# Router logits from four column groups and heads' squares added by GpSimd in the mix stage of an encoder layer

## The chip, the cores and the metric

One Trainium2 chip, of which the kernel uses one core. The metric is device time in microseconds (us) of one execution. TensorE works through matrix products, VectorE and ScalarE through elementwise work, GpSimd through elementwise work beside them, SyncE issues most transfers. TensorE's clock has two levels, 1.2 and 2.4 GHz; the profile gives the granted clock as a share of the upper one.

## The reference, cut to what matters

One layer of a hybrid encoder: 1024 tokens of 1024 channels, three mixers (Hyena, RG-LRU, 8 heads of attention), whose outputs are normalised, joined and projected; a residual and a layer norm; then 16 experts, each of which picks its best 128 tokens.

```python
y = concatenate([_rms_norm(y_hy, gn[:g0]), _rms_norm(y_lr, gn[g0:g1]), _rms_norm(y_at, gn[g1:])], axis=-1)
x = _layer_norm(alpha * x + y @ w_out[l], ln_mix_g[l], ln_mix_b[l])
...
affinity = softmax(einsum("bsd,de->bse", x, router_w), axis=-1)   # 1024 channels to 16 experts
gate, idx = top_k(swapaxes(affinity, 1, 2), cap)
```

The change touches the second and the fourth of these lines: how the mean square of the heads' output `y_at` is formed, and how the logits `x @ router_w` are.

## The kernel before

The program is one block for each engine, written in order by hand, with semaphores between the engines. No scheduler moves anything. Memory is one arena with places by number.

The **mix stage** goes over the 1024 tokens in 8 tiles of 128 (`for i in range(TT)` in each engine's block). For tile i TensorE does, in this order:

- 24 products of 128x512 for the Hyena and LRU channels into banks 0 and 1 (L1516 to L1518, `mix`). Each fp32 product is made of three products of rounded halves (high x high, high x low, low x high), so 4 slices x 2 halves of the columns x 3.
- the turning of the finished row of tile i-1 (`x1_turn`, L1494, 8 transposes into banks 4 and 5).
- the sum of squares of the heads' output of tile i: four fp32 products of the squares `o_sq` (128 x 128 each) with a column of ones into column i of bank 7 (L1539).
- 24 products for the heads' channels into banks 2 and 3 (`mix` again).
- the router logits of tile i-1 (`logits`, L1507): 8 fp32 products with the turned row `x1T` as weights (128 columns) and 16 moving columns of the router's matrix `rw`.

An fp32 product stands as two records in the trace, a rounded one as one.

ScalarE makes the rounded high part of the heads' output of tile i+2 and its squares (`heads_out`, L949 and L950), the roots, the router's exponential, the copies of turned rows, and starts the accumulator. GpSimd multiplies and shifts the residual row of the tile (`residual`, L619 and L620, after its transfer has landed) and forms the low part of the heads' output (`heads_out_low`, L613). VectorE adds the residual to banks 0 and 1 (L2033), adds the heads' banks 2 and 3 scaled (L2046; L2057 in two halves for the last tile), takes the statistics, and applies the norm in two steps with a tensor from memory each (L2052 with the gain, L2053 with the shift). The finished row x1 goes to memory and to `x1_turn`, and only after it does SyncE issue the transfer of the residual row two tiles on (L514). Since the buffers are double, tile i+1's residual follows tile i-1's finished row.

In the last tile the heads' products come in two halves of the columns, and its logits follow the turning of its row. Then VectorE picks the tokens (about 37 us) and the experts begin.

Of the kernel before, what the change touches and what calls it, by code (L numbers as in the profile page):

```python
# [8 lines left out]
ALU = mybir.AluOpType  # L9
ACT = mybir.ActivationFunctionType  # L10
# [71 lines left out]
def encoder(nc, A, out):  # L82

    ctx = ExitStack()
    with ctx:
        def sem(name):
            return ctx.enter_context(nc.semaphore(name))
# [134 lines left out]
        rw = mem(52176, KT, NE)  # L222
# [57 lines left out]
        s_x1st, s_acst, s_acc = [sem(f"x1_stored{i}") for i in range(2)], [sem(f"acc_stored{i}") for i in range(2)], sem("acc_scaled")  # L280
        s_x1p, s_x1ta, s_x1tv, s_lg = sem("x1_turned"), sem("x1T_act"), sem("x1T_dve"), sem("logits")
# [115 lines left out]
        def _(sp):  # L397
# [98 lines left out]
            sp.dma_start(rw, rows(A["router_w"][0])).then_inc(s_rw, 16)  # L496
# [44 lines left out]
        def _(pool):  # L541
# [72 lines left out]

            def residual(i):

                res = xres[:, i % 2, :]
                pool.wait_ge(s_xh[i % 2], 32 + 16 * (i // 2 + 1))
                link(pool.tensor_tensor(res, res, gin, ALU.mult))  # L619
                pool.tensor_tensor(res, res, bin_, ALU.add).then_inc(s_res, 1)  # L620

            pool.wait_ge(s_gb, 32)
            residual(0)
            heads_out_low(0)
            heads_out_low(1)
            residual(1)
            for i in range(2, TT):
                residual(i)
                heads_out_low(i)

# [56 lines left out]
        def _(act):  # L687
# [283 lines left out]

            def mix_root(i):

                act.wait_ge(s_st, TT + i + 1)
                a(sd[:, i % 2:i % 2 + 1], mv[:, i % 2, 1:2], ACT.Sqrt, bias=eps).then_inc(s_sd, 1)
# [10 lines left out]
            for i in range(TT):  # L986
                if i:
                    x1_copy(i - 1)
                heads_root(i)
                if i >= 2:  # L990
                    router_exp(i - 2)
                if i + 2 < TT:
                    heads_out(i + 2)
                mix_root(i)
                if i + 1 < TT:
                    acc_start(i)
# [65 lines left out]
        def _(pe):  # L1062
# [433 lines left out]

            def logits(i):

                if i == 0:
                    pe.wait_ge(s_rw, 48 + 16)  # L1500
                else:
                    pe.wait_ge(s_re, i)
                pe.wait_ge(s_x1ta, i + 1)
                for k in range(KT):
                    if k == KT // 2:
                        pe.wait_ge(s_x1tv, i + 1)
                    ins = mm(bank(6)[:, NE * (i % 2):NE * (i % 2) + NE], x1T[i % 2][:, P * k:P * k + P], rw[:, k, :], start=(k == 0), stop=(k == KT - 1))  # L1507
                ins.then_inc(s_lg, 1)
# [16 lines left out]
            for i in range(TT):  # L1525
# [7 lines left out]
                pe.wait_ge(s_sq, SUMS + i + 1)  # L1533
# [4 lines left out]
                for c in range(4):  # L1538
                    ins = mm(bank(7)[:, i:i + 1], o_sq[:, i % 2, c, :], ones[:, 0:1], start=(c == 0), stop=(c == 3))  # L1539
                ins.then_inc(s_ssq, 1)  # L1540
# [3 lines left out]
                if i + 1 < TT:  # L1544
                    for c in range(4):
                        ins = mix(2, 4 + c, ya_hi[:, i % 2, c, :], ya_lo[:, i % 2, c, :], c == 0, c == 3)
                    ins.then_inc(s_mix, 1)
                else:
                    for j in range(2):
                        for c in range(4):  # L1550
                            ins = mix_half(2, j, 4 + c, ya_hi[:, i % 2, c, :], ya_lo[:, i % 2, c, :], c == 0, c == 3)
                        ins.then_inc(s_mix, 1)
                if i:
                    logits(i - 1)
# [633 lines left out]
```

## Time and profile before

| | us |
|---|---|
| median of 3 runs | 1585.96 |
| lowest and highest | 1584.27, 1586.00 |
| the profiled execution, device time | 1584.54 |
| its span | 1582.7 |
| the mix stage in it | about 819 to 945 |
| the experts' stage in it | about 990 to the end |

Mean granted clock 0.98. TensorE is busy 95% of the span, VectorE 63%, ScalarE 46%, GpSimd 26%. In a timeline a row gives the start, the duration, the engine, the line and the operation; neighbours of one line are drawn together with their count, and the square bracket tells how long the engine was idle before and what ended that. Because records of TensorE overlap, the time of one is read from the distance of the starts. A record of VectorE or GpSimd includes what it waits for once it has begun.

### The profile page before, as it was taken

The page shows a single profiled execution, that of the slowest core. Times are in us where ns is not written, and L with a number is a line of the kernel's source. Part 1 is how long each engine was busy: PE and PEld are TensorE (multiplying, and loading weights), DVE is VectorE, ACT ScalarE, POOL GpSimd, SP SyncE. Part 2 cuts the span into 40 slices and gives each one's busy share as a digit, 9 for nine tenths or more (in the row PEclk, how much of TensorE's full clock was granted, in tenths as well). Part 3 has the DMA queues.
Part 4 walks back from the last instruction along what each step waited for, and adds up shares of the span by engine and source line. Part 5 has one row for each costly group of instructions (what it writes and reads, how often), then busy time and mean ns, then how long its engine had stood idle before and what let it go on. Part 6 is the DMA issues. An engine that isn't in the chain of part 4 may idle for free.

```text
span 1582.7 us, 15796 instructions
## 1 busy us (share of the span) xinstructions
PE 1497.3 (95%) x5862; PEld 996.5 (63%) x5862; DVE 1003.1 (63%) x1014; ACT 720.9 (46%) x696; POOL 406.3 (26%) x209
## 2 busy tenths in 40 slices
PE   6999999999999999999999970999999999999997
PEld 3444487844344444555558860788888888888774
DVE  4533244442842564655635558699989989998886
ACT  3301000025422114355443341677777777777773
POOL 0031000000011003576673414023322223332204
PEclk9999999999999999999999985999999999999999
DMA  9311030115100000000123249699999999999994
GB/s 315 131 54 53 25 135 1 33 31 116 53 0 1 0 0 27 1 27 1 54 82 104 96 156 378 235 368 377 378 371 375 378 378 378 378 379 368 377 381 195
DMA packets 152886, 284.46 MB, mean 180 GB/s; under 512 B 25300, under 2 KB 35874, under 8 KB 152835
## 3 DMA queue, kind: packets, MB, share of 16 engines
q1 hardware_dynamic: 147219, 263.32, 46.8%
q0 software_dynamic: 4464, 16.25, 3.9%
q10 hardware_dynamic: 1152, 4.19, 0.6%
q8 instruction: 34, 0.56, 0.1%
q14 instruction: 17, 0.14, 0.0%
HBM read 259.10 MB, written 24.64 MB: 179 GB/s over the span
## 4 chain that ended last, share of the span: by engine, by line
PE 85%; DVE 6%; DMA 4%; ACT 2%; issue 2%; POOL 1%; SPq 0%; POOLq 0%; DVEq 0%; ACTq 0%
PE psum L1145 14%; PE psum L1605 9%; PE psum L1607 9%; PE psum L1606 9%; PE psum L1376 4%; PE psum L1238 3%; PE psum L1126 3%; DMA arena<-in_exp_w_down 3%; PE psum L1438 3%; PE psum L1346 3%; PE psum L1426 2%; PE psum L1091 2%; PE psum L1449 2%; PE psum L1427 2%; PE psum L1428 2%; PE psum L1254 2%
## 5 line engine op out<-in xcount | busy, mean ns | idle before, releaser
L2109 DVE TENSOR_TENSOR split_at<-arena,split_at 128x2048 fp32r<-128x2048 f32 x188 | 427.9, 2290 | 60.6 <-ACT split_at L1007 59.7
L1007 ACT ACTIVATE split_at<-arena 128x2048 fp32r<-128x2048 f32 x192 | 367.6, 1915 | 68.5 <-PE psum L1607 53.3
L1605 PE MATMUL psum<-split_at,split_at 128*128 128x512 f32 x768 | 305.9, 398 | 1.4 <-DVE split_at L2115 1.4
L1607 PE MATMUL psum<-split_at,split_at 128*128 128x512 f32 x768 | 300.2, 391 | 0.0
L1606 PE MATMUL psum<-split_at,split_at 128*128 128x512 f32 x768 | 299.5, 390 | 0.0
L1145 PE MATMUL psum<-arena 128*128 128x512 f32 x512 | 224.7, 594 | 1.4 <-DVE arena L1862 1.4
L1145 PEld LDWEIGHTS psum<-arena 128*128 128x128 f32 x512 | 96.1, 190 | 124.0 <-issue 123.9
L1607 PEld LDWEIGHTS psum<-split_at,split_at 128*128 128x128 f32 x768 | 144.5, 188 | 31.2
L1605 PEld LDWEIGHTS psum<-split_at,split_at 128*128 128x128 f32 x768 | 144.7, 188 | 29.7 <-DVE split_at L2115 1.8
L1606 PEld LDWEIGHTS psum<-split_at,split_at 128*128 128x128 f32 x768 | 144.9, 189 | 28.3
L1920 DVE TENSOR_REDUCE arena<-psum 128x1 f32<-128x1024 f32 x64 | 78.1, 1224 | 68.9 <-PE psum L1346 68.2
L639 POOL COPY arena<-arena 128x1 uint32 (+1 forms) x14 | 28.3, 2020 | 359.4 <-DVE arena L2143 359.4
L582 POOL TENSOR_TENSOR arena<-arena 128x1024 f32<-128x1024 f32 x32 | 75.6, 2371 | 170.2 <-ACT arena L889 133.2
L889 ACT ACTIVATE arena<-psum 128x1024 f32<-128x1024 f32 x64 | 65.4, 1022 | 71.4 <-PE psum L1428 71.2
L1376 PE MATMUL psum<-arena 128*128 128x512 f32 x176 | 77.0, 592 | 0.0
L1012 ACT ACTIVATE split_at<-psum 128x512 fp32r<-128x512 f32 x64 | 38.2, 597 | 74.8 <-PE psum L1574 61.6
L1438 PE MATMUL psum<-arena 128*64 128x512 f32 x256 | 60.9, 596 | 0.0
L558 POOL TENSOR_TENSOR arena<-arena 128x1024 f32<-128x1024 f32 x7 | 16.8, 2394 | 167.2 <-ACT arena L816 160.7
L1376 PEld LDWEIGHTS psum<-arena 128*128 128x128 f32 x176 | 33.3, 190 | 40.0 <-issue 39.3
L657 POOL DMA_INDIRECT acc_scratch<-arena x15 | 50.9, 3391 | 28.1 <-DVE arena L2143 25.7
L1238 PE MATMUL psum<-arena 128*128 128x256 f32 x256 | 57.5, 379 | 0.0
L761 ACT ACTIVATE arena<-psum 128x256 f32<-128x256 f32 x8 | 3.1, 383 | 117.0 <-PE psum L1254 103.0
(302 smaller groups left out, 2219.3 us busy)
## 6 DMA issues: line engine op xcount, KB each, us to landing
arena<-in_exp_w_gate SPq DMA_DIRECT2D x64, 1024.0 KB, 14.4
arena<-in_exp_w_up SPq DMA_DIRECT2D x64, 1024.0 KB, 14.2
arena<-in_exp_w_down SPq DMA_DIRECT2D x64, 1024.0 KB, 14.4
arena<-in_w_in SPq DMA_DIRECT2D x9, 1024.0 KB, 8.4
arena<-in_x SPq DMA_DIRECT2D x8, 512.0 KB, 6.6
xhat_scratch<-arena SPq DMA_DIRECT2D x8, 512.0 KB, 10.0
arena<-in_w_out SPq DMA_DIRECT2D x8, 512.0 KB, 3.6
arena<-xhat_scratch SPq DMA_DIRECT2D x8, 512.0 KB, 4.8
```

Source lines behind the costliest of these rows:

```text
L582: pool.tensor_tensor(p_pair[q % 2], p_at[:, b, :], p_at[:, b + 1, :], ALU.add).then_inc(s_pa, 1)
L889: a(p_at[:, n % 4, :], bank(2 * (n % 2), 2), ACT.Exp).then_inc(s_exp, 1)
L1007: a(flat(wsplit[c % WS][0]), wraw[:, c], ACT.Copy).then_inc(s_whi, 1)
L1145: ins = mm(bank(proj_bank(i) + j, 1, p0, p0 + w), win_w[c][:, k, at:at + w], xT[:, k, HALF * j:HALF * j + HALF], start=(k == 0), stop=(k = ...
L1238: ins = mm(bank(4 + f % 2)[:, HYW * part:HYW * part + HYW], mat[:, i, P * f:P * f + P], pm[:, part, i, :], start=(i == 0), stop=(i == 3))
L1376: ins = mm(bank(heads_bank(u) + j), w[:, k, P * i:P * i + P], src[:, k, HALF * j:HALF * j + HALF], start=(k == 0), stop=(k == n_k - 1))
L1438: ins = mm(bank(6, 1, DV * j, DV * j + DV), v_at[:, kb, DV * h:DV * h + DV], p_at[:, n % 4, HALF * j:HALF * j + HALF], start=(kb == 0), st ...
L1605: mm(bank(out_bank), src[0][:, k, :], whi[:, k % 4, :], start=(k == 0), stop=False)
L1606: mm(bank(out_bank), src[0][:, k, :], wlo[:, k % 4, :], start=False, stop=False)
L1607: ins = mm(bank(out_bank), src[1][:, k, :], whi[:, k % 4, :], start=False, stop=(k == KT - 1))
L1920: v.tensor_reduce(nm[:, h % 2, qt:qt + 1], bank(b, 2), AX.X, ALU.max, negate=True).then_inc(s_nm, 1)
L2109: tt(flat(lo), wraw[:, c], flat(hi), ALU.subtract).then_inc(s_wlo, 1)
```

## The change

- **Squares.** GpSimd adds the four slices of `o_sq` of each tile to one, in two instructions (`add_heads_squares`: 256 columns, then 128). It does so right after the tile's low part. TensorE's sum of squares is then one product in place of four, and waits for GpSimd in place of ScalarE.
- **Logits of tiles 0 to 6.** The router's matrix is kept with 32 columns for each slice (16 of them zero). TensorE takes it as weights, and the turned row moves (128 columns). Slice k goes to column group k % 4, so that bank 7 holds, on four times 32 partitions, four parts of the transposed logits (`logit_parts`). This stands in the middle of the heads' products of the tile after. ScalarE copies the 128x128 of parts (`logit_copy`) ahead of its `heads_out`. One product with the copy as weights and a table that holds four identity matrices (`lg_sum`) adds the parts and turns them (`logits_of_parts`), where the logits stood.
- **The last tile's logits** stay as they were.
- GpSimd clears `rw` once ahead of the stage, and SyncE loads `lg_sum` (128x32) behind the router's matrix.

```diff
-            sp.dma_start(rw, rows(A["router_w"][0])).then_inc(s_rw, 16)
+            sp.wait_ge(s_zero, 2)
+            sp.dma_start(rw[:, :, 0:NE], rows(A["router_w"][0])).then_inc(s_rw, 16)
+            sp.dma_start(lg_sum, A["c_rot"][:, P:P + DR]).then_inc(s_rw, 16)
...
+            def add_heads_squares(i):
+
+                pool.wait_ge(s_sq, SUMS + i + 1)
+                o = o_sq[:, i % 2]
+                link(pool.tensor_tensor(o[:, 0:2], o[:, 0:2], o[:, 2:4], ALU.add))
+                pool.tensor_tensor(o[:, 0], o[:, 0], o[:, 1], ALU.add).then_inc(s_sqa, 1)
...
+            pool.wait_ge(s_qro, 2)
+            pool.memset(rw, 0.0).then_inc(s_zero, 1)
             pool.wait_ge(s_gb, 32)
             residual(0)
             heads_out_low(0)
+            add_heads_squares(0)
             heads_out_low(1)
             residual(1)
+            add_heads_squares(1)
             for i in range(2, TT):
                 residual(i)
                 heads_out_low(i)
+                add_heads_squares(i)
...
+            def logit_copy(i):
+
+                act.wait_ge(s_lp, i + 1)
+                if i >= 2:
+                    act.wait_ge(s_lg, i - 1)
+                a(lg_part[:, i % 2, :], bank(7)[:, P + P * (i % 2):2 * P + P * (i % 2)], ACT.Copy).then_inc(s_lc, 1)
...
                 if i >= 2:
                     router_exp(i - 2)
+                if i:
+                    logit_copy(i - 1)
                 if i + 2 < TT:
                     heads_out(i + 2)
...
+            def logit_parts(i):
+
+                if i == 0:
+                    pe.wait_ge(s_rw, 48 + 32)
+                if i >= 2:
+                    pe.wait_ge(s_lc, i - 1)
+                pe.wait_ge(s_rsd, ROOTS + i + 2)
+                pe.wait_ge(s_x1ta, i + 1)
+                pe.wait_ge(s_x1tv, i + 1)
+                for k in range(KT):
+                    p0 = DR * (k % 4)
+                    ins = mm(bank(7, 1, p0, p0 + DR)[:, P + P * (i % 2):2 * P + P * (i % 2)], rw[:, k, :], x1T[i % 2][:, P * k:P * k + P],
+                             start=(k < 4), stop=(k >= 4))
+                ins.then_inc(s_lp, 1)
+
+            def logits_of_parts(i):
+
+                pe.wait_ge(s_lc, i + 1)
+                if i:
+                    pe.wait_ge(s_re, i)
+                mm(bank(6)[:, NE * (i % 2):NE * (i % 2) + NE], lg_part[:, i % 2, :], lg_sum[:, 0:NE], start=True, stop=True).then_inc(s_lg, 1)
...
-                pe.wait_ge(s_sq, SUMS + i + 1)
+                pe.wait_ge(s_sqa, 7 + i + 1)
...
-                for c in range(4):
-                    ins = mm(bank(7)[:, i:i + 1], o_sq[:, i % 2, c, :], ones[:, 0:1], start=(c == 0), stop=(c == 3))
-                ins.then_inc(s_ssq, 1)
+                mm(bank(7)[:, i:i + 1], o_sq[:, i % 2, 0, :], ones[:, 0:1], start=True, stop=True).then_inc(s_ssq, 1)
...
                     for c in range(4):
+                        if i and c == 2:
+                            logit_parts(i - 1)
                         ins = mix(2, 4 + c, ya_hi[:, i % 2, c, :], ya_lo[:, i % 2, c, :], c == 0, c == 3)
...
                 if i:
-                    logits(i - 1)
+                    logits_of_parts(i - 1)
```

On TensorE, after the Hyena and LRU products of a tile, before: the turning (L1494), the squares (L1539) and the first of the heads' products.

```order
1392 L1494 MATMUL psum<-arena 128x128 [waits x1T_act,x1_done]
1393 L1494 MATMUL psum<-arena 128x128 x3
1394 L1494 MATMUL psum<-arena 128x128 [waits x1T_dve,x1_done]
1395 L1494 MATMUL psum<-arena 128x128 x3
1396 L1539 MATMUL psum<-arena 128x1 [waits rms_root,squares]
1397 L1539 MATMUL psum<-arena 128x1 x3
1398 L1516 MATMUL psum<-split_at_1024_58,heads_out_high 128x512 [waits mix_read,heads_out_split]
```

The same place in the changed kernel (its L1519, L1584 and L1560 are those three).

```order
1383 L1519 MATMUL psum<-arena 128x128 [waits x1T_act,x1_done]
1384 L1519 MATMUL psum<-arena 128x128 x3
1385 L1519 MATMUL psum<-arena 128x128 [waits x1T_dve,x1_done]
1386 L1519 MATMUL psum<-arena 128x128 x3
1387 L1584 MATMUL psum<-arena 128x1 [waits rms_root,logit_parts_copied,squares_added]
1388 L1560 MATMUL psum<-split_at_1024_58,heads_out_high 128x512 [waits mix_read,heads_out_split]
```

One product of squares stands there in place of four, and it waits for GpSimd's `squares_added`.

On TensorE, around the end of the heads' products, before: the logits (L1507) between them and the next tile's Hyena products.

```order
1420 L1517 MATMUL psum<-split_at_1024_52,heads_out_high 128x512
1421 L1518 MATMUL psum<-split_at_1024_52,heads_out_low 128x512
1422 L1507 MATMUL psum<-arena 128x16 [waits x1T_act,router_exp]
1423 L1507 MATMUL psum<-arena 128x16 x3
1424 L1507 MATMUL psum<-arena 128x16 [waits x1T_dve]
1425 L1507 MATMUL psum<-arena 128x16 x3
1426 L1516 MATMUL psum<-split_at_1024_54,hyena_high 128x512 [waits mix_read_first]
```

In the changed kernel: the parts (L1533) in the middle of the heads' products, and the product that adds them (L1542) behind.

```order
1399 L1562 MATMUL psum<-split_at_1024_59,heads_out_low 128x512
1400 L1533 MATMUL psum<-arena 32x128 [waits x1T_act,x1T_dve,rms_root,logit_parts_copied]
1401 L1533 MATMUL psum<-arena 32x128 x7
1402 L1560 MATMUL psum<-split_at_1024_50,heads_out_high 128x512
...
1413 L1562 MATMUL psum<-split_at_1024_52,heads_out_low 128x512
1414 L1542 MATMUL psum<-arena 128x16 [waits router_exp,logit_parts_copied]
1415 L1560 MATMUL psum<-split_at_1024_54,hyena_high 128x512 [waits mix_read_first]
```

Eight products left the place between two tiles, eight narrower ones stand inside the heads' products, and one is left between the tiles.

On GpSimd, from one tile's low part to the next, before.

```order
83 L613 TENSOR_TENSOR heads_out_low<-arena,heads_out_high 128x512 [waits mix_psum,heads_out_high]
84 L619 TENSOR_TENSOR arena<-arena 128x1024 [waits x_ld1]
85 L620 TENSOR_TENSOR arena<-arena 128x1024 [waits pool_chain]
86 L613 TENSOR_TENSOR heads_out_low<-arena,heads_out_high 128x512 [waits mix_psum,heads_out_high]
87 L619 TENSOR_TENSOR arena<-arena 128x1024 [waits x_ld0]
```

The same in the changed kernel.

```order
88 L617 TENSOR_TENSOR heads_out_low<-arena,heads_out_high 128x512 [waits mix_psum,heads_out_high]
89 L623 TENSOR_TENSOR arena<-arena 128x256 [waits squares]
90 L624 TENSOR_TENSOR arena<-arena 128x128 [waits pool_chain]
91 L630 TENSOR_TENSOR arena<-arena 128x1024 [waits x_ld0]
92 L631 TENSOR_TENSOR arena<-arena 128x1024 [waits pool_chain]
93 L617 TENSOR_TENSOR heads_out_low<-arena,heads_out_high 128x512 [waits mix_psum,heads_out_high]
```

The two adds stand between the low part and the next tile's residual.

## Rows read from the trace of the kernel before

**Rows 1.** Busy time by stretch: PE, PEld, DVE, ACT, POOL, then granted clock, DMA

```profile
838.00:931.00 93.00, 92.95 (x512) 79.86 (x513) 51.81 (x82) 38.32 (x61) 36.09 (x18) 1.00 0.35 114
```

**Rows 2.** TensorE's waits, 815 to 945 us: total, times, longest

```profile
PE psum L1494 <- DVE arena L2053: 0.8, 1, 0.8
```

**Rows 3.** Timeline of one tile, TensorE's weight loads: start, duration

```profile
867.95 0.97 PEld L1539 LDWEIGHTS psum<-arena 128*128 128x128 f32 x8
...
868.84 0.19 PEld L1516 LDWEIGHTS psum<-split_at,heads_out_high 128*128 128x128 f32 x1
...
874.22 1.98 PEld L1507 LDWEIGHTS psum<-arena 128*128 128x128 f32 x16
...
876.11 0.19 PEld L1516 LDWEIGHTS psum<-split_at,hyena_high 128*128 128x128 f32 x1
```

**Rows 4.** Timeline of VectorE's head-sums and norms, and TensorE's wait

```profile
831.98 1.28 DVE L2046 SCALAR_TENSOR_TENSOR arena<-psum,arena 128x1024 f32<-128x1024 f32 x1 [5.71 <-PE psum L1518]
...
835.39 1.28 DVE L2052 SCALAR_TENSOR_TENSOR arena<-arena 128x1024 f32<-128x1024 f32 x1
836.71 1.28 DVE L2053 SCALAR_TENSOR_TENSOR arena<-arena 128x1024 f32<-128x1024 f32 x1
...
838.05 1.09 PE L1494 MATMUL psum<-arena 128*128 128x128 f32 x8 [0.78 <-DVE arena L2053]
...
845.64 1.28 DVE L2046 SCALAR_TENSOR_TENSOR arena<-psum,arena 128x1024 f32<-128x1024 f32 x1 [5.18 <-PE psum L1518]
...
918.59 1.28 DVE L2046 SCALAR_TENSOR_TENSOR arena<-psum,arena 128x1024 f32<-128x1024 f32 x1 [3.30 <-PE psum L1518]
...
933.05 0.75 DVE L2057 SCALAR_TENSOR_TENSOR arena<-psum,arena 128x512 f32<-128x512 f32 x1 [1.14 <-PE psum L1518]
```

**Rows 5.** Products with 32 weight columns: counts and starts by line, then the timeline

```profile
L1160 PE MATMUL psum<-arena x32: 592/592/617, 394.9 to 401.4; 128*32 128x512 f32 x32
...
L1172 PE MATMUL psum<-arena x8: 589/589/613, 417.4 to 420.5; 64*32 64x512 f32 x8
...
394.93 0.14 PEld L1160 LDWEIGHTS psum<-arena 128*32 128x32 f32 x4 [0.76 <-issue]
...
401.92 0.30 PEld L1284 LDWEIGHTS psum<-arena 128*128 128x128 f32 x2 [0.84 <-issue]
```

**Rows 6.** Timeline of GpSimd at the stage's start and in a later tile

```profile
824.81 2.50 POOL L613 TENSOR_TENSOR heads_out_low<-arena,heads_out_high 128x512 fp32r<-128x512 f32 x2
...
826.13 0.50 PE L1516 MATMUL psum<-split_at,heads_out_high 128*128 128x512 f32 x1 [0.48 <-POOL heads_out_low L613]
...
843.45 2.39 POOL L619 TENSOR_TENSOR arena<-arena 128x1024 f32<-128x1024 f32 x1 [11.31 <-DMA arena<-xhat_scratch]
...
894.22 1.28 DVE L2053 SCALAR_TENSOR_TENSOR arena<-arena 128x1024 f32<-128x1024 f32 x1
...
900.61 2.39 POOL L619 TENSOR_TENSOR arena<-arena 128x1024 f32<-128x1024 f32 x1 [7.51 <-DMA arena<-xhat_scratch]
...
905.41 1.30 POOL L613 TENSOR_TENSOR heads_out_low<-arena,heads_out_high 128x512 fp32r<-128x512 f32 x1
```

**Rows 7.** Timeline where GpSimd and VectorE meet, and L2052's group over the stage

```profile
864.93 1.28 DVE L2053 SCALAR_TENSOR_TENSOR arena<-arena 128x1024 f32<-128x1024 f32 x1
...
873.31 2.38 POOL L619 TENSOR_TENSOR arena<-arena 128x1024 f32<-128x1024 f32 x1 [10.05 <-DMA arena<-xhat_scratch]
...
878.12 1.29 POOL L613 TENSOR_TENSOR heads_out_low<-arena,heads_out_high 128x512 fp32r<-128x512 f32 x1
878.15 2.34 DVE L2052 SCALAR_TENSOR_TENSOR arena<-arena 128x1024 f32<-128x1024 f32 x1
...
1066.64 4.48 DVE L2109 TENSOR_TENSOR split_at<-arena,split_at 128x2048 fp32r<-128x2048 f32 x2
1066.86 2.10 POOL L639 COPY arena<-arena 128x1 uint32<-128x1 uint32 x1 [25.79 <-DVE arena L2143]
...
L2052 DVE SCALAR_TENSOR_TENSOR arena<-arena 128x1024 f32<-128x1024 f32 x7 | 10.4, 1481 | 0.2
```

More of the change, by code:

```diff
@@ L221, in encoder @@
         x1T = [mem(43984, D), mem(45008, D)]
-        rw = mem(52176, KT, NE)
+        rw, lg_part = mem(52176, KT, DR), mem(52432, 2, P)
+        lg_sum = mem(432, DR)
         accb = mem(46032, 2, D)
@@ L280, in encoder @@
         s_x1st, s_acst, s_acc = [sem(f"x1_stored{i}") for i in range(2)], [sem(f"acc_stored{i}") for i in range(2)], sem("acc_scaled")
+        s_lp, s_lc = sem("logit_parts"), sem("logit_parts_copied")
         s_x1p, s_x1ta, s_x1tv, s_lg = sem("x1_turned"), sem("x1T_act"), sem("x1T_dve"), sem("logits")
@@ L1495, in x1_turn @@
                     ins.then_inc(s_x1p, 1)
+            def logit_parts(i):
[16 more added lines that the diff above has]
+                mm(bank(6)[:, NE * (i % 2):NE * (i % 2) + NE], lg_part[:, i % 2, :], lg_sum[:, 0:NE], start=True, stop=True).then_inc(s_lg, 1)
             def logits(i):
[L1499 to L1502, printed above, removed]
+                pe.wait_ge(s_re, i)
                 pe.wait_ge(s_x1ta, i + 1)
@@ L1506, in logits @@
                         pe.wait_ge(s_x1tv, i + 1)
-                    ins = mm(bank(6)[:, NE * (i % 2):NE * (i % 2) + NE], x1T[i % 2][:, P * k:P * k + P], rw[:, k, :], start=(k == 0), stop=(k == KT - 1))
+                    ins = mm(bank(6)[:, NE * (i % 2):NE * (i % 2) + NE], x1T[i % 2][:, P * k:P * k + P], rw[:, k, 0:NE], start=(k == 0), stop=(k == KT - 1))
                 ins.then_inc(s_lg, 1)
@@ L1532, in _ @@
                     x1_turn(i - 1)
-                pe.wait_ge(s_sq, SUMS + i + 1)
+                pe.wait_ge(s_sqa, 7 + i + 1)
+                if i >= 2:
+                    pe.wait_ge(s_lc, i - 1)
                 if i == 0:
@@ L1549, in _ @@
                     for j in range(2):
+                        if j:
+                            logit_parts(i - 1)
                         for c in range(4):
```

## The prediction

> **What bounds the kernel now.** I read first the busy time of the engines by stretch, then the waits in the mix stage, then the timeline of one token tile. The change touches one stage only: the output projection, residual, layer norm and router, from about 819 to 945 us. There TensorE is busy all the time at the full granted clock [rows 1], and in the tiles before the last it waits for VectorE once, 0.8 us [rows 2]. One tile takes the time from one head-sum (L2046, it starts 0.13 us after the tile's last product) to the next. The first interval is 845.64 - 831.98 = 13.66 us. The five after it take (918.59 - 845.64)/5 = 14.59 us each, and the last 933.05 - 918.59 = 14.46 [rows 4]. The six after the first sum to 87.41 us.
>
> The first interval is shorter because no router logits lie in it, and it shows what stands close behind TensorE. VectorE runs from the head-sum of a tile to its finished row (L2053 ends 836.71 + 1.28 = 837.99), 6.01 us, and TensorE, which then has only the 24 products of the next tile's Hyena and LRU parts (5.38 us, as the 24 of the heads in [rows 3]), waits 0.78 us to turn that row [rows 4]. In the later intervals the logits, 1.89 us, lie between and hide the VectorE chain. **So what the logits give back is paid out only down to that chain.** Call T the end of L2053.
>
> **Part by part.** *Squares.* Eight records of L1539 take 868.84 - 867.95 = 0.89 us, 0.112 each. One product is two records, 0.22. Gain 0.67 us a tile on TensorE [rows 3].
>
> *Logits.* Sixteen records of L1507 take 876.11 - 874.22 = 1.89 us, set by loading 128 columns of weights [rows 3]. They go. The product that adds the parts is two such records, 0.22 us. It stands where TensorE will be waiting for the row to turn, so it costs nothing while that wait is over 0.2 us, and 7 x 0.22 = 1.5 us if it is gone.
>
> *Parts.* Sixteen records with 32 weight columns and 128 moving ones, in four column groups, stand inside the heads' products. Is this cheap? The nearest row is the key projection L1160, which is built the same way with two groups: 32 records from 394.9 to 401.4, that is 6.5/31 = 0.21 us a record of 512 columns. The single-group L1172 needs 3.1/7 = 0.43 us [rows 5]. So groups run at once; 128 columns alone would be 0.107 us. Four weight loads of 32 columns fit in 0.14 us [rows 5], so loading doesn't bound it. With four groups at once, 16 records are 4 x 0.107 = 0.43 us. Going between the modes costs: L1160's last record starts 401.4, lasts 0.43 by its rate, and the next full-width load starts only at 401.92, then its 0.11 us is bare; about 0.09 in, 0.20 out [rows 5]. Sum 0.43 + 0.29 + some stagger = **0.77 us**. Bounds: 0.6, and 16 x 0.107 + 0.3 = 2.0 if the groups don't overlap. I take 0.77, as L1160 shows the overlap with two.
>
> ScalarE gets one more 128x128 copy between the router's exponential and the next tile's heads. Only the adding product waits for it, behind 12 further products of the heads (2.7 us), and the turning products of the next tile don't.
>
> *The new interval, without contention.* From T: turning and squares in the first interval take from 838.05 to the head-sum at 845.64. So the next head-sum is at T + 7.65 - 0.67 + 0.77 = T + 7.75, and the next T is 6.01 later: **13.76 us**. TensorE's own work would be 14.59 - 0.67 - 1.89 + 0.22 + 0.77 = 13.02, so VectorE's chain is the bound, with 0.7 us of waiting on TensorE.
>
> *The adds on GpSimd.* They are 128x256 and 128x128. From 1.29 us for 512 columns and 2.39 for 1024 [rows 6] the time is 0.2 + 2.13 ns a column: 0.75 and 0.47, with the link between 1.29 us a tile. They matter in two places.
>
> First, at the start. Now the low part of tile 0 ends at 824.81 + 1.25 = 826.06 and the heads' products begin at 826.13, after a wait of 0.48 [rows 6]. Then the adds follow that low part, and TensorE must take the squares' product before the heads: adds to 827.3, product to 827.6. Nothing hides it: **+1.45 us**.
>
> Second, the port that VectorE and GpSimd share. GpSimd's low part ran 878.12 to 879.41, and the norm's L2052, begun at 878.15, took 2.34 instead of 1.28 us: it finished 1.08 after GpSimd was done [rows 7]. The reverse shows too: GpSimd's 128x1 copy took 2.10 us under VectorE's L2109 and ended when that ended, though VectorE had another queued right behind it [rows 7]. So one instruction at a time, and who waits gets in at the boundary. The Trainium skill, page "SBUF — State Buffer", section "SBUF: two separate sides", speaks against the adds: the pair of ports that both use is an exclusive lock, held by the one that starts first for its whole instruction, and the other blocks fully. By that rule alone each collision costs what is left of an instruction, up to rival C's total; without it rival A's total would stand. The trace agrees, by the 2.34 us.
>
> Where will they fall? GpSimd's residual starts when its transfer has landed: 900.61 against T = 895.50, 5.11 after; 843.45 against 837.99, 5.46 after; once 873.31 against 866.21, 7.10 after [rows 4, 6, 7]. The low part ends 6.10 us after that start [rows 6], at T + 11.2 to 11.6. The norm's L2052 is wanted 3.41 us after the head-sum [rows 4], at T + 11.16, and L2053 at T + 12.48. So L2052 gets in at the end of the low part (0 to 0.2 us late). The first add waits for it and gets in before L2053, which costs 0.75 less what is prepared while waiting, 0.3 to 0.5 us. I take **0.45 us** a tile for both, over the six intervals that have such an overlap. Ends: 0, if VectorE takes both norms together, and 1.1, if GpSimd keeps the port for the low part and the first add and takes it again for the second. One late transfer of the seven would then cost about 1 us, where before it cost 0.15; I put 0.5.
>
> **The sum.** Start +1.45; first interval 13.76 - 13.66 = +0.10; six intervals 6 x 13.76 - 87.41 = -4.85; contention 6 x 0.45 = +2.7; a late transfer +0.5. Total -0.1 us. The last tile's logits, the choice of tokens and the experts have the same instructions, and the end of the stage waits for VectorE's last row as before. The memset stands where GpSimd waits for the first row's transfer, and the 16 KB transfer where SyncE's queue has nothing until the first finished row: nothing. The profiled execution took 1584.54 us, 1.4 under the median of 1585.96; against the median the forecast is **1585.9 us, no change that can be measured** (about 0.2%, 3.2 us, is what a measurement can tell here).
>
> **The rivals.** *A, the port doesn't collide.* If VectorE's norms go through back to back, or GpSimd's work is early, the 2.7 and 0.5 fall away: -3.3 us, 1582.7. With parts at 0.6 it is -4.5, 1581.5. For it: the seven L2052 of the stage lost only 10.4 - 7 x 1.28 = 1.4 us in all [rows 7]. Against: the norms come 0.7 us earlier in the interval, and GpSimd has 1.3 us more right there. Chance 0.22, half of it beyond 0.2%.
>
> *B, slower: the column groups don't overlap four ways.* With fp32's two passes a group, perhaps only two run at once: parts 1.2 us. That adds 7 x 0.43 = 3.0, the contention stays near 0.45, and the sum is +2.9, 1588.9. With no overlap parts are 2.0: +8.6, while the norms fall behind the adds (T + 12.4 against T + 12.5) and contention drops to 0.1, -2.1: +6.4, 1592.4. The point is a parts time of about 1.25 us, from which the change loses over 0.2%. For it: no row has four groups. Against: two groups overlap fully. Chance 0.13.
>
> *C, slower: GpSimd wins the port twice.* Contention 1.1 a tile: 6 x 0.65 = +3.9 over the forecast, 1589.7. It turns on who is served at a boundary; the copy's row speaks against it. The same end comes if more transfers are late, 1 us each. Chance 0.12.
>
> *D, it doesn't do what it says:* TensorE stays the bound, since the turned row is never late. Then intervals are 13.02: another 7 x 0.74 = -5.2, less the contention, which is then hidden: about -8.5, 1577.5. The 0.78 us wait with no logits ahead of it speaks against it. Chance 0.03.
>
> **How the numbers follow.** The forecast's own case has 0.50; A 0.22, B 0.13, C 0.12, D 0.03. The range takes in A and the near ends of B and C, with some of B's far end: 1582.0 to 1591.0. Faster by over 0.2%: half of A and D, 0.14. Slower: most of B and C, 0.22. Within: 0.64.
>
> **What would show it.** In the changed profile: L1539's successor two records a tile; the parts 16 records in about 0.77 us with starts in fours; a wait of TensorE for the norm before each turning of 0.5 to 1.2 us; the first heads' products 1.4 us later than before; norms of 1.5 to 2 us where GpSimd's adds run beside them, and a GpSimd add stretched over 1 us. Intervals of 14.0 to 14.4 us confirm the sum; 13.7 would be A, 14.6 and more B or C. The prediction is wrong outright if something outside the mix stage moves by over 1 us.

## The result and the profile after

The changed kernel takes **1586.91 us** (median of 20 runs, 1585.66 to 1589.58); the kernel before took 1585.12 on the same chips (20 runs, 1581.95 to 1586.19). The ratio is 1.0015, with a 95% interval of 1.0008 to 1.0022: 1.3 to 3.5 us slower. The ratio itself is still inside the 0.2% that I had called no change. The prediction was 0.1 us faster. So the change was forecast 2 to 2.5 us too low (the medians differ by 1.8 us, the ratio makes 2.4), and its sign is wrong, by an amount that the interval excludes. In the ratios of this document, runs that took over 1.5% more than the fastest of their kernel are left out: one of e6 and one of e9 below.

The mix stage first by stretch of the changed kernel, with the columns of [rows 1]; the second line answers to that row:

```profile
817.00:838.00 21.00, 18.47 (x76) 14.53 (x73) 10.83 (x17) 5.44 (x10) 14.28 (x10) 0.92 0.22 67
838.00:931.00 93.00, 85.76 (x500) 67.33 (x500) 55.30 (x85) 38.64 (x68) 51.47 (x30) 1.00 0.35 114
```

In the same 93 us TensorE was busy for 92.95 - 85.76 = 7.2 us less, and GpSimd for 51.47 - 36.09 = 15.4 us more. So TensorE, which set the stage's pace before, now stands idle for 7 us of it. TensorE's waits over the stage (engine, line, what it waited for: total, times, longest) say for what:

```profile
PE psum L1519 <- DVE arena L2101: 7.2, 7, 1.2
...
PE psum L1584 <- POOL arena L624: 2.5, 1, 2.5
```

Against [rows 2] the wait for the norm has gone from 0.8 us once to 7.2 us in seven tiles: most of the work that was removed came back as waiting for VectorE. The second line is new, once, at the start of the stage. VectorE's rows, which answer to [rows 4]:

```profile
833.37 1.28 DVE L2094 SCALAR_TENSOR_TENSOR arena<-psum,arena 128x1024 f32<-128x1024 f32 x1 [6.82 <-PE psum L1562]
...
847.22 1.28 DVE L2094 SCALAR_TENSOR_TENSOR arena<-psum,arena 128x1024 f32<-128x1024 f32 x1 [5.36 <-PE psum L1562]
...
919.18 1.28 DVE L2094 SCALAR_TENSOR_TENSOR arena<-psum,arena 128x1024 f32<-128x1024 f32 x1 [3.39 <-PE psum L1562]
...
933.50 0.75 DVE L2105 SCALAR_TENSOR_TENSOR arena<-psum,arena 128x512 f32<-128x512 f32 x1 [1.91 <-PE psum L1562]
```

The first interval is 847.22 - 833.37 = 13.85 us (13.66 before), the six after it sum to 933.50 - 847.22 = 86.28 (87.41 before). So the intervals gave back 0.94 us, where 1.55 were forecast (2.05 without the 0.5 for a late transfer, which didn't come). The first head-sum is 15.97 us behind the stage's first product (817.40, L1560), where it was 12.92 before (831.98 less 819.06): 3.05 us lost, where 1.45 were forecast. The stage is 2.1 us longer in this execution.

One later tile in detail, VectorE and GpSimd as in [rows 7] (start, duration):

```profile
878.33 1.29 POOL L617 TENSOR_TENSOR heads_out_low<-arena,heads_out_high 128x512 fp32r<-128x512 f32 x1
...
879.12 1.58 DVE L2100 SCALAR_TENSOR_TENSOR arena<-arena 128x1024 f32<-128x1024 f32 x1
...
879.58 1.72 POOL L623 TENSOR_TENSOR arena<-arena 128x256 f32<-128x256 f32 x1
...
880.74 1.64 DVE L2101 SCALAR_TENSOR_TENSOR arena<-arena 128x1024 f32<-128x1024 f32 x1
...
881.37 1.32 POOL L624 TENSOR_TENSOR arena<-arena 128x128 f32<-128x128 f32 x1
```

The two engines take strict turns. The low part ends at 879.62, and the first norm, which was issued under it, ends 1.08 us later, at 880.70. The first addition, issued under that norm, ends 0.60 later, at 881.30; the second norm 1.08 after it, at 882.38; the second addition 0.31 after it. The norms take 3.22 us together instead of 2.57. This is the port rule of the Trainium skill (page "SBUF — State Buffer", section "SBUF: two separate sides": one holder for a whole instruction, the other blocked), and the trace agrees: the 128-column addition took 1.32 us here and 0.45 where nothing ran beside it. The rule doesn't say who comes next; these rows do: the one that waits.

The stage's start, TensorE and GpSimd, which answers to [rows 6]:

```profile
823.14 1.27 POOL L617 TENSOR_TENSOR heads_out_low<-arena,heads_out_high 128x512 fp32r<-128x512 f32 x1
...
824.36 0.72 POOL L623 TENSOR_TENSOR arena<-arena 128x256 f32<-128x256 f32 x1
...
825.17 0.45 POOL L624 TENSOR_TENSOR arena<-arena 128x128 f32<-128x128 f32 x1
...
825.67 0.38 PE L1584 MATMUL psum<-arena 128*128 128x1 f32 x2 [2.53 <-POOL arena L624]
...
826.70 0.48 PE L1560 MATMUL psum<-split_at,heads_out_high 128*128 128x512 f32 x1
...
827.83 0.63 PE L1560 MATMUL psum<-split_at,heads_out_high 128*128 128x512 f32 x1
...
829.11 0.63 PE L1560 MATMUL psum<-split_at,heads_out_high 128*128 128x512 f32 x1
```

Of the products one in three stands here. The additions take 0.72 and 0.45 us, as worked out, and TensorE waits 2.53 us. But the rows at 827.83 and 829.11 are 1.28 us apart, 0.43 a product, and elsewhere a product takes 0.23. The windows of this stretch (the granted clock is third from the end) show why:

```profile
815.00:826.00 11.00, 8.47 (x39) 5.32 (x35) 6.50 (x10) 4.08 (x6) 8.87 (x8) 1.00 0.50 152
826.00:830.00 4.00, 4.00 (x13) 3.11 (x13) 0.16 (x1) 0.26 (x1) 3.92 (x3) 0.61 0.00 0
830.00:838.00 8.00, 8.00 (x36) 6.67 (x35) 4.17 (x6) 1.45 (x3) 2.80 (x3) 0.98 0.00 0
```

Just behind the wait the granted clock fell from 2.4 to 1.2 GHz: 0.39 x 4 us and 0.02 x 8 us are missing, at half each, so for (1.56 + 0.16)/0.5 = 3.4 us. No term of the prediction has this. Yet the trace of the kernel before shows such a fall, at the end of the stage: after a wait of 2.31 us for the last tile's norm, and another of 0.79, its clock was at half too.

```profile
937.01 0.66 PE L1494 MATMUL psum<-arena 128*128 128x128 f32 x4 [2.31 <-DVE arena L2071]
```

```profile
937.00:938.00 1.00, 0.66 (x4) 0.42 (x4) 0.96 (x2) 0.29 (x1) 0.00 (x0) 1.00 0.00 0
...
940.00:942.00 2.00, 2.00 (x12) 2.00 (x11) 0.80 (x2) 0.00 (x0) 0.00 (x0) 0.50 0.89 231
```

### The profile page after: what moved, and what is told of

It reads as the page before. It is cut to its first block, busy times and chain, and to the rows that moved or that the text cites. A ratio compares the mean times of both kernels' runs of the same rounds, so it can differ in the third digit from the quotient of the medians.

```text
span 1585.8 us, 15771 instructions
## 1 busy us (share of the span) xinstructions
PE 1488.3 (94%) x5828; PEld 982.7 (62%) x5828; DVE 1004.6 (63%) x1014; ACT 722.8 (46%) x703; POOL 424.3 (27%) x226
## 4 chain that ended last, share of the span: by engine, by line
PE 82%; DVE 8%; DMA 4%; ACT 2%; issue 2%; POOL 1%; SPq 0%; POOLq 0%; DVEq 0%; ACTq 0%
PE psum L1170 14%; PE psum L1653 9%; PE psum L1655 9%; PE psum L1654 9%; PE psum L1401 4%; PE psum L1263 3%; PE psum L1151 3%; DMA arena<-in_exp_w_down 3%; PE psum L1463 3%; PE psum L1371 2%; PE psum L1451 2%; PE psum L1116 2%; PE psum L1474 2%; PE psum L1452 2%; PE psum L1453 2%; PE psum L1279 2%
```

## The experiments

All numbers are of the stage, from its first product (s0) over the first head-sum (H0) to the last tile's second head-sum (H7; the last tile's comes in two halves of the columns). "Norms" is the busy time of the seven pairs, 18.0 us where nothing disturbs them. The ratio is to runs of the kernel before, made beside each kernel on the same chip.

| kernel | H0 - s0 | H7 - H0 | norms | PE waits for norm | us | ratio, 95% |
|---|---|---|---|---|---|---|
| before | 12.92 | 101.07 | 19.4 | 0.8 | | |
| changed | 15.97 | 100.13 | 21.3 | 7.2 | 1586.91 | 1.0015, 1.0008 to 1.0022 |
| e1: tile 0 as before | 12.97 | 99.42 | 20.6 | 6.5 | 1584.20 | 1.0000, 0.9991 to 1.0009 |
| e2: logits alone | 12.89 | 102.08 | 18.6 | 4.5 | 1586.00 | 1.0011, 1.0002 to 1.0020 |
| e4: additions behind the norm | 16.01 | 96.76 | 18.0 | 3.9 | 1583.51 | 0.9995, 0.9986 to 1.0004 |
| e5: squares at tile 0 alone | 14.29 | 100.93 | 18.0 | 0.8 | 1586.73 | 1.0015, 1.0006 to 1.0025 |
| e6: e1 and e4 | 12.89 | 96.82 | 18.0 | 3.9 | 1581.51 | 0.9978, 0.9969 to 0.9987 |
| e7: squares from tile 1 alone | 12.88 | 98.35 | 25.1 | 1.6 | 1581.32 | 0.9977, 0.9968 to 0.9986 |
| e8: e6, parts moved | 12.90 | 91.80 | 18.8 | 1.4 | 1576.27 | 0.9945, 0.9933 to 0.9957 |
| e9: one column group | 14.44 | 106.18 | 18.6 | 2.6 | 1593.51 | 1.0055, 1.0042 to 1.0068 |

e1, e2, e4 and e5 shared one chip, with the kernel before at 1584.27 us (33 runs), e6 to e9 another, at 1584.79 (23 runs). The differences of times follow those of the stage within 2.1 us. In eight of the nine kernels the time is on the slow side of what the stage gives. What lies outside the stage moves by a microsecond or more from execution to execution, and about one may belong to the new logits (below).

### The start: tile 0's additions

e1 leaves the change as it is but for tile 0:

```diff
             heads_out_low(0)
-            add_heads_squares(0)
             heads_out_low(1)
...
+                if i:
+                    pe.wait_ge(s_sqa, 7 + i)
+                else:
+                    pe.wait_ge(s_sq, SUMS + 1)
...
+                n_sq = 1 if i else 4
```

> The changed kernel, with tile 0 alone as before: TensorE sums its four slices of squares itself and doesn't wait for GpSimd. Theory S (the start costs 3.0 us: 1.4 of waiting for the adds and 1.6 because the granted clock falls to half for 3.4 us behind that wait): no half-clock stretch at 826 us, first head-sum 3.0 us earlier against the end of the scores' stage, time 1583.9. Rival R (the loss is in the tiles' intervals, the norms stretched by GpSimd's adds, and the start matters by its wait alone): 1585.4. The seven intervals themselves stay at 13.85 and 14.4 us by both.

The first head-sum came at 12.97 us, as before, and TensorE's wait at the start fell from 2.53 to 0.50 us. The time is that of the kernel before (1.0000). So without tile 0's additions the change isn't slower. Against 1.0015 they cost some 2.4 us, with intervals too wide to choose between theory S (3.0) and rival R (1.5). What they cost has two parts, which the next kernels tell apart. e5 puts the same additions, and the one product, at tile 0 into the kernel before, and nothing else of the change:

```diff
             heads_out_low(0)
+            add_heads_squares(0)
             heads_out_low(1)
...
+                added = i == 0
+                if added:
+                    pe.wait_ge(s_sqa, 7 + i + 1)
+                else:
+                    pe.wait_ge(s_sq, SUMS + i + 1)
...
+                n_sq = 1 if added else 4
```

> The kernel before, with the change's adds and its single product of squares in tile 0 alone; all else as before. Theory S: TensorE waits about 2.5 us ahead of the first heads' products, the granted clock falls to half for 3.4 us, and the time is 3.0 over the kernel before, 1588.1. Rival R (the clock's fall was a chance of one execution): 1.4 over, 1586.5.

```profile
828.28 0.45 POOL L620 TENSOR_TENSOR arena<-arena 128x128 f32<-128x128 f32 x1
...
828.78 0.38 PE L1552 MATMUL psum<-arena 128*128 128x1 f32 x2 [2.44 <-POOL arena L620]
...
829.81 0.39 PE L1524 MATMUL psum<-split_at,heads_out_high 128*128 128x512 f32 x1
...
830.50 0.39 PE L1524 MATMUL psum<-split_at,heads_out_high 128*128 128x512 f32 x1
```

These are GpSimd's last addition and TensorE behind it, in e5. The wait is the same 2.4 us, but the products stay 0.23 us apart, and the head-sum is 14.29 us behind s0: +1.37, where the prediction's term was +1.45. So the wait itself was worked out rightly, and what came on top in the changed kernel is the fall of the clock. (e5's time, 1.0015, is 2.4 us over the kernel before, between its two theories. Only one of its 11 runs was profiled, so how many of them had a fall isn't known.) Does that belong to the change? Three more executions, of the changed kernel twice and of e5 once, all unaltered:

> The changed kernel unaltered, in one more profiled execution. In the first one the granted clock was 0.61 over 826 to 830 us, just behind TensorE's 2.5 us wait for the last square of tile 0, and the first head-sum started 15.97 us behind the first heads' product. Theory A (the fall of the clock belongs to this kernel: the wait makes it) expects the fall again, the head-sum at 15.9 to 16.1. Theory B (the same wait is followed by a fall in some executions alone, as in the kernel that has the change at tile 0 only, which waited 2.4 us and kept 1.00) expects some executions with 14.3 to 14.4 and no fall. The seven intervals behind it: both 14.2 to 14.5.

> The same kernel once more, with the same two theories: A expects the granted clock to fall behind the wait and the first head-sum 15.9 to 16.1 us behind the first heads' product; B expects one of the executions to show 14.3 to 14.4 with the clock at 1.00.

> The kernel before with the change at tile 0 alone (GpSimd's additions and one product against ones), unaltered, in one more profiled execution. TensorE waits 2.4 us for GpSimd's last addition. Theory A (the fall of the clock belongs to the changed kernel and not to this one, whatever in it differs ahead of the wait) expects the granted clock at 1.00 and the head-sum 14.3 us behind the first heads' product again. Theory B (chance of the execution) allows a fall here too, with 15.9.

Windows of the changed kernel's two executions, first the one with the fall, then the one without (columns as above, the clock is third from the end):

```profile
826.00:830.00 4.00, 4.00 (x12) 3.09 (x12) 0.16 (x1) 0.20 (x1) 3.92 (x3) 0.57 0.00 0
```

```profile
826.00:830.00 4.00, 3.36 (x16) 2.81 (x17) 0.17 (x1) 0.26 (x1) 3.92 (x4) 1.00 0.00 0
```

The same kernel, behind the same wait (2.5 and 2.6 us), fell in the first (head-sum 16.03 us behind s0) and not in the second (14.46). Theory B holds: the fall comes in some executions of one kernel and not in others. It costs 16.03 - 14.46 = **1.6 us** when it comes. Over all kernels with this wait it came in three of seven profiled executions (the changed kernel twice in three, e4 once) and stayed away in four (the changed kernel, e5 twice, e9). In the three with a fall the stage had begun at 817.2 to 817.4 us, in the four without at 818.3 to 820.6; whether that decides, these runs don't tell. In before, e1, e2, e6, e7 and e8, whose waits there are 0.5 us or less, it didn't come here in the one profiled execution of each.

### The port: additions against the norms

e2 keeps the new logits and takes the additions away from all tiles:

```diff
-            add_heads_squares(0)
...
-            add_heads_squares(1)
...
-                add_heads_squares(i)
...
-                pe.wait_ge(s_sqa, 7 + i + 1)
+                pe.wait_ge(s_sq, SUMS + i + 1)
...
+                for c in range(4):
```

> The changed kernel without GpSimd's adds: four products of squares a tile on TensorE as before, the logits by column groups kept. Expected: norms (the two steps with gain and shift) back at 1.28 us each, interval 7.80 + 0.67 + 6.01 = 14.48 us, first one 0.8 us longer than before, six others 0.1 each shorter, start as before: 1585.4, the same as the kernel before. Rival (the stretched norms don't come from the adds but from the low part): norms still 0.4 to 0.7 us long together, intervals of 14.9, 1588.

The norms came down from 21.3 to 18.6 us, so the additions account for 2.7 of the 3.3 us by which they were stretched; the low part, which meets two of them, makes the rest. And **the new logits alone made the stage longer**, by 1.0 us, because the intervals are bound by the VectorE chain and the parts stand on it: 14.51 us in the plain intervals, against 14.56 before, and 14.50 in the first against 13.66. TensorE waited 4.5 us for the norm. The time says the same with less certainty: 1.0011, where no change was expected. e4 keeps everything, and from tile 2 on GpSimd does the low part and the additions only behind the finished row of the tile two before, and the residual after them:

```diff
             for i in range(2, TT):
-                residual(i)
+                pool.wait_ge(s_x1, i - 1)
                 heads_out_low(i)
                 add_heads_squares(i)
+                residual(i)
```

> The changed kernel, with GpSimd's order altered for tiles 2 to 7: it waits for the finished row of the tile two before, then does the low part and the adds, and only then the residual, so that nothing of GpSimd's runs beside the norm. If the adds beside the norm cost 0.56 us in each of six tiles: norms 1.28 us, intervals 13.8, time 1586.9 - 3.4 = 1583.5, with the start still 3.0 us late. Rival: the waits of TensorE stay because GpSimd's work now comes too late for the squares: a wait of TensorE for the adds in each tile and no gain.

The groups of the two norms and the two additions over the stage (busy, mean ns of one | idle before), first in the changed kernel, then in e4:

```profile
L2100 DVE SCALAR_TENSOR_TENSOR arena<-arena 128x1024 f32<-128x1024 f32 x7 | 11.0, 1572 | 0.2
...
L2101 DVE SCALAR_TENSOR_TENSOR arena<-arena 128x1024 f32<-128x1024 f32 x7 | 10.3, 1473 | 0.2
...
L623 POOL TENSOR_TENSOR arena<-arena 128x256 f32<-128x256 f32 x8 | 8.9, 1116 | 0.0
...
L624 POOL TENSOR_TENSOR arena<-arena 128x128 f32<-128x128 f32 x8 | 8.8, 1105 | 0.6
```

```profile
L2101 DVE SCALAR_TENSOR_TENSOR arena<-arena 128x1024 f32<-128x1024 f32 x7 | 9.0, 1285 | 0.2
...
L2102 DVE SCALAR_TENSOR_TENSOR arena<-arena 128x1024 f32<-128x1024 f32 x7 | 9.0, 1285 | 0.3
...
L623 POOL TENSOR_TENSOR arena<-arena 128x256 f32<-128x256 f32 x8 | 5.9, 741 | 0.0
...
L624 POOL TENSOR_TENSOR arena<-arena 128x128 f32<-128x128 f32 x8 | 3.7, 460 | 0.6
```

All seven norms are clean, 3.3 us shorter in sum, and H7 - H0 is 3.37 us shorter: contention, with the low part and the additions together, cost 0.56 us in each of the six tiles. The plain interval without it, which the prediction put at 13.76, is seen here:

```profile
874.78 1.28 DVE L2095 SCALAR_TENSOR_TENSOR arena<-psum,arena 128x1024 f32<-128x1024 f32 x1 [3.38 <-PE psum L1563]
...
879.51 1.28 DVE L2102 SCALAR_TENSOR_TENSOR arena<-arena 128x1024 f32<-128x1024 f32 x1
...
880.85 1.09 PE L1520 MATMUL psum<-arena 128*128 128x128 f32 x8 [0.52 <-DVE arena L2102]
...
888.59 1.28 DVE L2095 SCALAR_TENSOR_TENSOR arena<-psum,arena 128x1024 f32<-128x1024 f32 x1 [3.35 <-PE psum L1563]
```

From head-sum to finished row 880.79 - 874.78 = 6.01 us, as forecast; from there to the next head-sum 7.80, where 7.75 was forecast. e6 joins e1 and e4, with no new line:

> Both repairs together: tile 0 keeps its four products of squares, and from tile 2 on GpSimd does the low part and the adds behind the norm of the tile two before. All of the change's logits stay. Expected if the two losses (start, stretched norms) are all that there is: start 12.97 us from the stage's first product to the first head-sum, seven intervals of 13.83, stage 4.3 us shorter than before, time 4.3 us (0.27%) under the kernel before. Rival (a third loss behind the stage, in the experts, that comes with the column groups): stage 4.3 shorter, time only 3 us or less under it.

It measured 0.22% under the kernel before (1581.51 us), the stage 4.3 us shorter. The two repairs add up: 3.1 us at the start (against an execution with the fall, which is 1.6 of them), 3.3 in the intervals. The time gained 3.3 us by the medians and 3.5 by the ratio, which is between the 4.3 expected and the rival's 3 or less. So the rival, a loss behind the stage, isn't excluded by it.

e7 is the other half of the change, the squares without the new logits, on the kernel before:

```diff
             residual(1)
+            add_heads_squares(1)
             for i in range(2, TT):
                 residual(i)
                 heads_out_low(i)
+                add_heads_squares(i)
...
+                added = i >= 1
...
+                n_sq = 1 if added else 4
```

> The kernel before with GpSimd's adds and the single product of squares in tiles 1 to 7, the logits as before. If TensorE's work is the bound wherever the old logits cover VectorE's chain: intervals of 14.56 - 0.67 = 13.9 us, the norms stretched by 0.4 to 0.7 us but hidden behind the logits (TensorE waits for no norm), stage 4.7 us shorter, 1579.6. Rival (stretched norms are on the path here too): intervals 14.3, stage 2.3 shorter, 1582.

```profile
876.00 1.29 POOL L613 TENSOR_TENSOR heads_out_low<-arena,heads_out_high 128x512 fp32r<-128x512 f32 x1
...
876.37 2.00 DVE L2066 SCALAR_TENSOR_TENSOR arena<-arena 128x1024 f32<-128x1024 f32 x1
...
877.25 1.72 POOL L619 TENSOR_TENSOR arena<-arena 128x256 f32<-128x256 f32 x1
...
878.40 1.64 DVE L2067 SCALAR_TENSOR_TENSOR arena<-arena 128x1024 f32<-128x1024 f32 x1
...
879.04 1.32 POOL L620 TENSOR_TENSOR arena<-arena 128x128 f32<-128x128 f32 x1
```

The logits' 1.89 us hide much of the chain here, yet my 13.9 us intervals were too short: they came out between 14.08 and 14.64 (13.85 the last). Here the norms start soon after the low part has begun, 876.37 against 876.00, and pay for the low part and both additions: 3.51 to 3.97 us a pair instead of 2.57. The first interval, which has no collision, is 13.01, and the next 13.01 + 1.07 = 14.08, so the chain binds here too: the rival came closer, with 14.22 on the mean over the six. It still gains 0.23%, as much as e6.

### The parts: four groups, and where they stand

e9 gives the changed kernel one column group, all eight blocks summed in it (with it the copy and the adding product go down to 32 partitions; those lines aren't shown):

```diff
-                    p0 = DR * (k % 4)
+                    p0 = 0
...
-                             start=(k < 4), stop=(k >= 4))
+                             start=(k == 0), stop=(k == KT - 1))
```

> The changed kernel, with all eight products of the parts in one column group, the copy and the adding product over 32 partitions. If the groups run at once in the change: parts take 16 x 0.107 + 0.3 = 2.0 us here in place of 0.57 to the next product's start, intervals about 1.4 us longer, less the contention of the norms with the adds, which then falls mostly away: 6 us over the changed kernel. Rival (the change's parts gain nothing by groups, only by narrow weights): the same time as the changed kernel.

TensorE around the parts, in e9 and then in e8, whose parts are those of the change:

```profile
873.05 0.39 PE L1562 MATMUL psum<-split_at,heads_out_low 128*128 128x512 f32 x1
...
873.37 1.93 PE L1533 MATMUL psum<-arena 128*32 128x128 f32 x16
...
875.23 0.50 PE L1560 MATMUL psum<-split_at,heads_out_high 128*128 128x512 f32 x1
```

```profile
870.47 0.39 PE L1562 MATMUL psum<-split_at,heads_out_low 128*128 128x512 f32 x1
...
870.79 0.64 PE L1533 MATMUL psum<-arena 128*32 128x128 f32 x16
...
871.36 0.50 PE L1560 MATMUL psum<-split_at,hyena_high 128*128 128x512 f32 x1
...
871.70 0.40 PE L1561 MATMUL psum<-split_at,hyena_high 128*128 128x512 f32 x1
```

Sixteen records take 1.86 us in one group and 0.57 in four. Intervals are 15.10 against 13.85 in e6, 1.25 more. So the four groups overlap, and rival B is out. With the way in and out, the parts push two neighbours from 0.45 to 871.70 - 870.47 = 1.23 us apart: 0.78 us for all, where 0.77 was forecast.

e8 is e6 with the parts taken off VectorE's chain. They follow the heads' products, so the head-sum no longer waits for them, and the adding product goes ahead of the turning one tile later, where TensorE waited for the norm. ScalarE's copy of the parts moves behind its `heads_out` (those lines aren't shown):

```diff
+                if i >= 2:
+                    logits_of_parts(i - 2)
                 if i:
                     x1_turn(i - 1)
...
-                        if i and c == 2:
-                            logit_parts(i - 1)
...
                 if i:
-                    logits_of_parts(i - 1)
+                    logit_parts(i - 1)
+            logits_of_parts(TT - 2)
```

> As the kernel with both repairs, and the parts' products moved from the middle of the heads' products to behind them, where TensorE waits for the norm; the product that adds them stands after the next Hyena and LRU products, and ScalarE's copy behind its heads' copies. If VectorE's chain from head-sum to finished row is the bound and the 0.8 us of parts were on the path: intervals 13.1 us in place of 13.83, almost no wait of TensorE, stage 9.4 us shorter than before, time 1575. Rival (ScalarE's later copy or the router's exponential holds the product that adds): intervals 13.8 with a wait of TensorE before that product.

Its head-sums start at 844.94, 857.99, 870.99, 883.99 and 896.99: 13.0 us apart. That is TensorE's own work in a tile by the prediction's count, 13.02, and TensorE waits 1.4 us for norms in two tiles, where e6 waited 3.9 in seven. **This version takes 1576.27 us, 0.55% less than the kernel before** (0.9933 to 0.9957). It is the fastest kernel here. One interval was 13.78. The residual row had landed late there, and GpSimd's work on it met the norm (the prediction had the low part meet it after a late transfer):

```profile
898.98 2.40 POOL L631 TENSOR_TENSOR arena<-arena 128x1024 f32<-128x1024 f32 x1
...
900.40 2.06 DVE L2105 SCALAR_TENSOR_TENSOR arena<-arena 128x1024 f32<-128x1024 f32 x1
```

### What lies outside the stage

The changed kernel's two later executions were 1587.53 and 1584.42 us, 3.1 apart, with one and the same program. 1.0 us of it arose while the input was loaded (it was the faster execution that lost there), 1.6 was the fall of the clock, and 2.5 came from single waits of VectorE in the experts' loop near 1398 and 1434 us. The last are as large as the whole effect measured here, and come in one execution of this kernel and not in another. They are why one execution says little of the change.

One part doesn't come and go. From the end of GpSimd's last instruction to the end of the program there are 3.40 to 3.45 us in all nine profiled executions of kernels with the new logits, and 3.00 to 3.07 in all four without. In the changed kernel and in the one before it is 1585.8 - 1582.38 = 3.42 and 1582.7 - 1579.70 = 3.00, by these rows:

```profile
1580.04 2.34 POOL L699 TENSOR_TENSOR arena<-arena 128x1024 f32<-128x1024 f32 x1 [0.48 <-ACT arena L1083]
```

```profile
1577.36 2.34 POOL L683 TENSOR_TENSOR arena<-arena 128x1024 f32<-128x1024 f32 x1 [0.48 <-ACT arena L1058]
```

From H7 to the end the nine took 651.1 us on the mean (649.8 to 652.3), the four 649.9 (649.3 to 650.9). So the new logits may cost about 1 us behind the stage, of which 0.4 is seen in every execution. What causes it isn't known.

## Why the prediction was wrong

The mechanism inside the stage was right but for what follows the wait at the start, and the sum of small terms missed its sign. By the prediction's own steps, for the stage, with the changed kernel's first execution, which had the fall, and (in brackets) the one without:

| term | forecast | measured |
|---|---|---|
| start | +1.45 | +3.05 (+1.54) |
| first interval | +0.10 | +0.19 (+0.19) |
| six intervals, clean | -4.85 | -4.5 (e4: 96.76 - 13.82 = 82.94 against 87.41) |
| contention, six tiles | +2.7 | +3.3 (e4: 86.28 - 82.94) |
| a late transfer | +0.5 | none |
| sum | -0.1 | +2.1 (+0.5, read directly) |

- **The step that failed is the start.** The prediction priced TensorE's wait and nothing that the wait might set off. The wait was right to 0.1 us (e5: +1.37; the changed kernel without the fall +1.54). Behind it the granted clock fell in two of the changed kernel's three profiled executions, at 1.6 us each time. The term was given as a point, with no end above it for what follows a wait; that end was missing in the sum and in the range.
- **Contention was sized 0.1 us a tile too low.** The order of turns was forecast right (low part, first norm, first addition, second norm), and the added wait was put at 0.3 to 0.5. It measured 0.56 a tile, 0.36 to 0.71, since both norms pay: 0.29 us on the first and 0.19 on the second, on the mean over seven. That is +0.6 in the sum.
- **The clean interval** is 13.83 instead of 13.76, mostly by the 0.05 us between row and next head-sum: +0.4 in six.
- **The late transfer** didn't come in the changed kernel. In e8 it did once, at 0.78 us, where it met the residual and not the low part; that this is near the forecast's "about 1 us" is partly luck.
- **Outside the stage** the prediction put nothing, and named a shift of over 1 us there as a sign that it is wrong outright. That sign came true in the changed kernel's first execution: against the kernel before, the stage began 1.7 us sooner and what is behind H7 took 2.6 us more. It tells little alone, as two executions of the changed kernel differ nearly as much, but about 1 us behind the stage may be the new logits', as said above.
- *Parts* (0.78 against 0.77), *VectorE's chain* (6.01), *the wait for the norm* before each turning (7.2 us in seven; 0.5 to 1.2 each) and *the adding product, memset and transfer at nothing* are as forecast: no wait stands at them in the changed kernel.
- *Rivals.* A is out by the stretched norms; its price for a clean port, 3.2 us, is what e4 recovered (3.4). B is out by e9. C named contention of 1.1 a tile, twice what came. D, TensorE as the bound at 13.02, is out for this change, and became true in e8, where the parts were moved.

How the measured +1.8 us (+2.4 by the ratio) divides between the start, the intervals and what lies outside can't be settled. The stage gives +0.5 without the fall and +2.1 and +2.2 with it, +1.6 on the mean of the three, and three executions are few. Why the clock falls in one execution and not in another stays open. What is shown is that either repair alone takes the slowdown away: tile 0 without its additions gives 1.0000 (e1), GpSimd's work behind the norm 0.9995 (e4). So tile 0's additions are not its only cause, though alone, in the kernel before, they cost 0.15% (e5).

## What to carry to other kernels

When work is taken off the engine that looks busiest, ask first what stands close behind it, here 0.8 us. The new logits alone made the stage longer (e2), and with both repairs the whole change gained 3.3 us (e6). Putting the new products where that engine waited gained another 5.2 (e8). Additions given to an idle GpSimd are not free when VectorE has two long instructions due at that time: each turn costs both, so put them behind VectorE's pair, or see that they start there by a wait. An operation moved ahead of the first item of a pipeline has nothing to hide it: treat the first tile apart. And price what a wait may set off, where the kernel's own trace shows it: the fall of the clock behind the 2.31 us wait stood in the trace of the kernel before.

## What the runs showed of the hardware

- A 2.5 us wait of TensorE, behind a stage at the full granted clock, was followed by some 3.4 us at 1.2 GHz in three of seven profiled executions, and by nothing in the four others, with the same kernel among both.
- VectorE and GpSimd took turns at instruction boundaries in these rows, even where each had the next one ready: a 128x128 addition of 0.45 us took 1.32, a 128x256 one of 0.74 took 1.72, a 128x1024 norm of 1.28 took 2.06 in e8.
- Sixteen fp32 records with 32 weight columns and 128 moving ones took 0.57 us from start to the next start in four column groups, and 1.86 in one.
